# Taking 1/rms out of the input of a two-layer trunk's projections, on one Trainium2 core

## The reference, cut to what matters

```
h    = x * rsqrt(mean(x*x, axis=-1) + eps) * norm_w      # RMSNorm: one factor per row
proj = h @ w_in                                          # 1024 x 4160
p_rwkv, p_conv, p_moba, p_ret = split(proj)
y_rwkv = rwkv7_time_mix(...) * silu(gate)                # shifts p by one row, mixes, tanh/sigmoid
y_conv = B * conv3(C * h) * silu(gate)                   # three projections multiplied
y_moba = block attention(q, k, v) * silu(gate)           # softmax, T5 bias
y_ret  = retention(q, k, v), scaled by its own rms, * silu(gate)
x = x + concat(y) @ w_out                                # 1024 x 1024
```

## Time and profile before

| | |
|---|---|
| median of three executions | 649.53 us |
| the profiled execution: its own time | 649.84 us |
| its span, first to last instruction | 647.9 us |
| mean granted TensorE clock | 0.992 |
| TensorE matmul busy | 623.8 us (96%) |
| VectorE busy | 359.5 us (55%) |
| ScalarE busy | 255.0 us (39%) |
| GpSimd busy | 250.4 us (39%) |

### The profile page before, as it was taken

The page is one execution under the profiler, slowest core; times in us unless marked ns, Lnnn a source line. Parts: engine busy times, 40 slices in busy tenths (PEclk is TensorE's granted clock), DMA queues, the critical chain, the costliest instruction groups (busy, mean ns, idle before and its releaser), DMA issues.

```text
span 647.9 us, 11976 instructions
## 1 busy us (share of the span) xinstructions
PE 623.8 (96%) x4939; PEld 495.9 (77%) x4939; DVE 359.5 (55%) x615; ACT 255.0 (39%) x491; POOL 250.4 (39%) x192
## 2 busy tenths in 40 slices
PE   4999999999999999999999999999999999999994
PEld 3777878888877776878877787888787777687884
DVE  4838965441148557783262896645123765688433
ACT  4463422432135436443345442242213535534421
POOL 3663644315513123446515353431461313154620
PEclk9999999999999999999989999999999999999997
DMA  8775633327222121355543233241822122125503
GB/s 245 225 243 148 159 98 87 85 51 166 70 62 67 34 66 32 97 147 159 168 113 98 65 98 98 67 107 17 180 82 67 34 67 56 43 65 179 147 0 129
DMA packets 122615, 66.76 MB, mean 103 GB/s; under 512 B 31359, under 2 KB 115907, under 8 KB 122435
## 3 DMA queue, kind: packets, MB, share of 16 engines
q1 hardware_dynamic: 122562, 66.02, 37.8%
HBM read 55.78 MB, written 10.22 MB: 102 GB/s over the span
## 4 chain that ended last, share of the span: by engine, by line
PE 90%; DVE 3%; ACT 2%; DMA 2%; issue 1%; SPq 0%; DVEq 0%; ACTq 0%
PE bank L663 24%; PE bank L664 22%; PE bank L665 22%; PE bank L808 3%; PE bank L761 2%; PE bank L822 2%; PE bank L849 2%; DMA pages<-in_x_dram 2%; PE bank L833 1%; PE bank L775 1%; DVE act_lo L1339 1%; PE bank L933 1%; PE bank L968 1%; PE bank L864 1%; PE bank L984 1%
## 5 line engine op out<-in xcount | busy, mean ns | idle before, releaser
L595 POOL TENSOR_TENSOR w_lo<-w_raw,w_hi 128x512 fp32r<-128x512 f32 x164 | 226.3, 1403 | 314.2 <-ACT w_hi L1062 314.2
L663 PE MATMUL bank<-act_hi,w_hi 128*128 128x512 f32 x656 | 267.2, 407 | 1.8 <-DVE act_lo L1665 1.3
L665 PE MATMUL bank<-act_lo,w_hi 128*128 128x512 f32 x656 | 256.1, 390 | 0.0
L664 PE MATMUL bank<-act_hi,w_lo 128*128 128x512 f32 x656 | 256.1, 390 | 0.0
L663 PEld LDWEIGHTS bank<-act_hi,w_hi 128*128 128x128 f32 x656 | 123.1, 188 | 40.7 <-issue 14.5
L665 PEld LDWEIGHTS bank<-act_lo,w_hi 128*128 128x128 f32 x656 | 123.1, 188 | 26.6
L664 PEld LDWEIGHTS bank<-act_hi,w_lo 128*128 128x128 f32 x656 | 123.4, 188 | 23.9 <-issue 1.4
L1062 ACT ACTIVATE w_hi<-w_raw 128x512 fp32r<-128x512 f32 x142 | 81.3, 622 | 51.4 <-PE bank L665 47.4
L1151 ACT ACTIVATE pages<-bank 128x512 f32<-128x512 f32 x24 | 14.4, 598 | 111.6 <-PE bank L665 111.6
L588 POOL TENSOR_TENSOR w_hi<-w_raw,constants 128x512 fp32r<-128x512 f32 x22 | 23.4, 1085 | 58.0 <-DMA w_raw<-in_w_in_dram 46.2
L1676 DVE TENSOR_TENSOR x_or_y<-x_or_y,bank 128x512 f32<-128x512 f32 x16 | 11.0, 688 | 37.6 <-PE bank L665 37.6
(11 more groups left out here) (178 smaller groups left out, 726.9 us busy)
## 6 DMA issues: line engine op xcount, KB each, us to landing
w_raw<-in_w_in_dram SPq DMA_DIRECT2D x66, 512.0 KB, 4.1
w_raw<-in_w_out_dram SPq DMA_DIRECT2D x16, 512.0 KB, 3.9
x_scratch<-x_or_y SPq DMA_DIRECT2D x16, 256.0 KB, 4.6
x_or_y<-x_scratch SPq DMA_DIRECT2D x16, 256.0 KB, 2.7
pages<-in_x_dram SPq DMA_DIRECT2D x4, 512.0 KB, 8.9
out_dram<-pages SPq DMA_DIRECT2D x4, 512.0 KB, 4.0
bias_scratch<-pages SPq DMA_DIRECT2D x1, 1280.0 KB, 7.4
constants<-in_consts_dram SPq DMA_DIRECT2D x1, 1064.5 KB, 6.5
```

The costliest lines, as they stand in the source:

```text
L595: ins = pool.tensor_tensor(w_lo[:, i % LO, k, :], w_raw[:, i % RAW, k, :], w_hi[:, i % HI, k, :].bitcast(F32), ALU.subtract)
L663: mm(b[:, :], hi, act_hi[:, k, :], start=n == 0, stop=False)
L664: mm(b[:, :], lo, act_hi[:, k, :], start=False, stop=False)
L665: ins = mm(b[:, :], hi, act_lo[:, k, :], start=False, stop=n == KT - 1)
```

## The change

The split tiles hold x * norm_w instead of x * norm_w * rn; every projection is multiplied by rn behind TensorE.

- The split (first layer): ScalarE writes act_hi, and VectorE act_lo, straight from the transposed tiles in PSUM, as soon as those are there. `keep_warm` is gone. The rms broadcast runs inside the k pair, ahead of its last products, and ScalarE copies it to SBUF (`rn`, a tile of its own).
- Between the layers: inside the step of out7, ScalarE and VectorE split x tiles 0 to 6 for the next layer while out7's matmuls run (out7 now takes its products in the order 0 to 7, and each frees its act tile); VectorE's 7 subtractions stand ahead of its addition of out7 in its list. The `stat` matmuls run inside the next k pair, after its fifth product.
- Behind the projections, a new VectorE instruction multiplies shift, gate, ch and cb tiles in PSUM, in place, ahead of their other readers: those tiles have 3 readers instead of 2. Tiles rq, rk, mk and cc are copied with that factor by VectorE and no longer by ScalarE. mq, mv and rv go on as plain ScalarE copies; their factor is put in the score scale (`q_scale`), in the copy of the transposed rows (8 instructions in place of 2), and in `k_decay_rms`.
- The steps `mix` and `gate_out` hold what `shift` and `gate` did last on VectorE.
- The constant `chunk_reset` (512 columns of 128 partitions) is no longer loaded; two memsets write it.

More of the change, by code:

```diff
@@ L226, in bank_jobs @@
         elif kind == "gate":
[L227 removed]
+            proj(f"{step[1]}_g{step[2]}", 3)
         elif kind == "kk_square":
@@ L383, in trunk_kernel @@
         mean_sq, root, rms = small[:, 8:12], small[:, 12:16], small[:, 16:20]
+        q_scale, k_decay_rms = small[:, 28:32], small[:, 32:48]
+        chunk_reset = half(13, 0)
         UW = pages[:, 21 * PG:21 * PG + 2048].rearrange("p (m x i) -> p m x i", m=MATS, x=2)
@@ L623, in _, with stat_both @@
                         end(ins, f"x_in{m}", -1)
+            def stat_both(layer):
+                stat(layer, False)
+                stat(layer, True)
             def stat(layer, last):
@@ L679, in project, with rms_row @@
                             product(job, n)
[L681 to L688, removed]
+                def rms_row():
                     pe.wait_ge(s("rms"), layer + 1)
@@ L1042, in _, with square_rows @@
                 .then_inc(done("norm_cols", -1), 1)
-            for t in range(NT):
+            def square_rows(t):
                 act.wait_ge(s(f"x_loaded{t}"), 16)
@@ L1166, in to_rows @@
                                 act.wait_ge(*read(f"ret_ms{1}", layer))
-                            go(rows[what][:, :, p * P:(p + 1) * P], src.rearrange("p (t c) -> p t c", t=NT), ACT.Copy).then_inc(done(job, layer), 1)
+                                for t in range(NT):
+                                    ins = go(rows[what][:, t, p * P:(p + 1) * P], src[:, t * P:(t + 1) * P], ACT.Copy, scale=rms[:, t:t + 1])
+                                ins.then_inc(done(job, layer), 1)
+                            else:
+                                go(rows[what][:, :, p * P:(p + 1) * P], src.rearrange("p (t c) -> p t c", t=NT), ACT.Copy).then_inc(done(job, layer), 1)
                 def inverse_x(n):
@@ L1331, in _ @@
             for layer in range(DEPTH + 1):
[L1332 to L1350 removed]
+                def norm():
                     if layer == 0:
                         derive()
+                    dve.wait_ge(s("rms"), layer + 1)
+                    ts(q_scale, rms, N ** -0.5, None, ALU.mult).then_inc(s("row_factors"), 1)
+                    tt(k_decay_rms.rearrange("p (h t) -> p h t", h=HEADS), const("k_decay").rearrange("p (h t) -> p h t", h=HEADS),
+                       rms.unsqueeze(1).to_broadcast([P, HEADS, NT]), ALU.mult).then_inc(s("row_factors"), 1)
                 def derive():
@@ L1679, in project_out @@
                             evacuate_row(n)
-                run = dict(norm=norm, shift=shift, kk_norm=kk_norm, decay_scan=decay_scan, factors=factors, bonus=bonus,
+                run = dict(norm=norm, shift=shift, mix=mix, copy=copy, gate_out=gate_out, kk_norm=kk_norm, decay_scan=decay_scan, factors=factors, bonus=bonus,
                            gate=gate, scores=scores, block_rows=block_rows, inverse_y=inverse_y, inverse_yt=inverse_yt, rotate=rotate,
```

138 lines of the change are left out of this document (79 added, 59 removed).

## The result

The changed kernel takes 660.56 us in the median (659.34 to 662.07, 4 runs) beside 649.75 (648.99 to 651.33, 4 runs) for the kernel before: ratio 1.0164 with a 95% interval of 1.0136 to 1.0193. It is slower, by 1.4 to 1.9%. Its profiled execution took 662.07 us with a span of 660.1; the span before was 647.9, so 12.2 us have to be found in the trace, of which 1.5 belong to this execution alone (it is that much above its median).

The account below looks back on a forecast made before the run. TensorE, its matmuls filling 96% of the span, was taken as the bound. Start -0.8, seam -1.7, mixing +10.1 and layer ends +1.6 gave +9.2 us on 649.84, 659.0; set against the median, 658.8 us, range 653.5 to 664.

Parts of the forecast that it names:

- Start: First k pair: begins earlier, but k1 waits for its low weights until 20.35 us; pair ends at 32.1, gain 0.8 us.
- Seam: Between the layers: k0 waits for out7's addition behind seven subtractions, TensorE still for 3.1 us; gain 1.7 us.
- then the pair 10.9: Layer 1's k pair, after out7's addition at the seam: takes 10.9 us.
- Mixing: Time-mixing part: VectorE late for banks, stalls of 1.05, 2.4, 0.85 and 0.75 us; 5.05 us a layer, 10.1 in both.
- lasts 5.07 as before: Time-mixing part: decay_scan starts at 60.7 us behind the lora tanh and takes 5.07 us, as before, until 65.8.
- Price of a multiplication: VectorE's added in-place multiplications in PSUM: 0.7 us each, ends 0.6 and 1.06.
- Rival C: VectorE's multiplications are dearer or cheaper than 0.7 us: 656 to 663 us, inside the range; no separate chance given.
- End of a layer: cb0, cb1, conv_g0 and conv_g1: added multiplications delay the split ahead of out0; cost 0.8 us a layer, 1.6 in both.
- Costed at nothing: Copies taken from ScalarE, mv's row copies, q_scale, k_decay_rms, memsets, block_rows, SP's weight loads: each under 1 us if uncovered.
- B: Time mixing: VectorE's chain is not late for banks 1 and 0, part costs under 1 us; 645 to 648 us, chance 0.08.
- D: Time mixing: only one of two large stalls comes, ScalarE's tanh not held up; about 654 us, chance 0.1.
- A: New idle stretches drop TensorE's clock: one drop 660.5 us, at most 0.45; three about 664; two or more 0.15.

Follow-up runs that it names:

- the eighth kernel: The changed kernel with the constant 0.125 in place of q_scale in the scores, leaving out the 1/rms of q: one run, 659.59 us.
- the whole repaired change: The changed kernel with VectorE's mixing list reordered, out7's addition after three subtractions and six idle passes at the start: 649.25 us, 0.9983 of the kernel before.
- the first kernel: The changed kernel with the seven shifted tiles multiplied into SBUF instead of in place, freeing PSUM after one reader: 667.12 us, ratio 1.0267.
- the fourth kernel: The changed kernel with ScalarE's four lora tanh moved ahead of its part of r1: one run, 665.14 us.

## Why the prediction was right

I said 658.8, 653.5 to 664.0, and 660.56 was measured. The sum came out from terms that were nearly all off, in both directions.

**Start: -0.8 said, +0.86 measured.** The pair's first product is at 17.34 (said 17.4) and k1's at 20.31 behind the low weights (20.35). In the execution of the eighth kernel, which has this start and kept the clock there, wa comes 0.98 us earlier than before. What I had only as a rival is the clock drop, 1.6 us.

**Seam: -1.7 said, +1.07 measured.** The mechanism is the one said: seven subtractions, then the addition. From the first to the addition behind them are 5.69 us instead of 5.2, and the idle is 3.6 instead of 3.1; that is the first subtraction's 1.78 us beside GpSimd, the others took the step that I had said. The failed step is "then the pair 10.9": it ran partly at half clock, 2.5 us. I had the drop at the seam of before in front of me and gave one drop at most 0.45 and more than one 0.15; two came.

**Mixing: 5.05 a layer said, 3.50 measured.** The four places are right: v1 0.89 (said 1.05), g0 1.57 (2.4), g1 0.33 (0.85), rq0 0.61 (0.75), rq1 0.10. The chain is right up to decay_scan, which starts 28.5 us behind the pair's end (said 28.6) and behind the held-up tanh. The step that failed is "lasts 5.07 as before": scaling and scans took 4.28 us. The scans are as long as before (3.39 us, 3.31 before); the scaling took 0.86 and not the 1.80 of the earlier trace rows, since GpSimd's pair ended 0.31 us after its start, while before it ran beside all of it (59.99 to 62.98). Likewise factors 0 took 4.48 and not 5.08: its first two instructions took 0.53 and 0.54 us with GpSimd still, 1.25 and 1.52 before. I had copied durations that a neighbour had stretched to a place where the neighbour stands elsewhere.

**Price of a multiplication: 0.7 said, 0.695 measured** (38 instructions in place in PSUM). Rival C falls away. Its upper end of 1.06 (5.29 / 5) was the mean of two kinds: three of those five subtractions took 0.68 us, the two that met GpSimd 1.79 and 1.78. The page's fifth part:

```profile
L1414 DVE TENSOR_TENSOR bank<-bank,one_over_rms 128x512 f32<-128x512 f32 (+1 forms) x38 | 26.3, 695 | 23.7 <-PE bank L679 23.2
```

**End of a layer: 0.8 said, 0.6 measured.**

**Costed at nothing: +1.2 us in layer 0 and +0.8 in layer 1.** I had looked at when block_rows' results are loaded, not at what stands behind it in VectorE's list: the multiplication of retention's second gate, then ScalarE's tanh of it and two weight splits, then the rows that TensorE needs for mq1, 0.7 us late (L970 waits for L1194). The other part, 0.53 in both layers, is the product beside GpSimd above. In layer 1 mq1 is only 0.13 us late, and 0.25 more, from cc0 to cc1, stay open.

**Rivals.** B (VectorE's chain not late) and D (one large stall only) did not come: both large stalls are there. A came with two drops, at 1.6 and 2.5 us. That it and the things costed at nothing were in part made up by a mixing term that was too large is luck: -3.1 (mixing, two layers), +1.7 and +2.8 (start and seam), +2.0 (costed at nothing), -0.4 (layer ends) is +2.9 before rounding on the sum of 9.2, and the profiled execution stands 1.5 above the median. What was right without luck is the sign and where the time went: over half of the 12.1 us lies in the mixing part, at the four places named. Bonus is at 90.00 us (said 90.1).

## What to carry to other kernels

A scale moved behind a linear step is not free because the engine that now applies it is half idle. It makes one more link between the bank's last matmul and its release, and where that engine works off a list without gaps, the tiles there pay (3.5 us over five tiles here, nothing for the many tiles where it waited); look at that stretch of its timeline and at the order of the list before counting its work. When banks are late, reorder the list before copying data out of PSUM: the copy moved the wait and made the readers dearer. And before rebuilding a seam to save its microseconds, see what the clock does in it: a handful of small matmuls in the waits of the kernel before gave as much as the whole repaired change.

## What was not expected of the hardware

A drop of TensorE's clock outlasts its cause, and its length changes from one execution to the next. Behind the wait for k1's weights, with the start's instructions unchanged, the clock stood at half rate for 3.4 us in three executions, for 6.8 in one and not at all in two. At the seam, behind 3.6 us of idle, it fell each time: for 6.8 us in three executions, where the changed kernel's pair lost 2.5 us by it, and for 3.4 in two.

VectorE's time for an instruction with two SBUF inputs depends on GpSimd beside it: 0.68 to 0.75 us alone, 1.71 and 1.77 when it started well before the end of a GpSimd instruction, 1.19 when it started near that end. It looks like waiting and not like a slower pace: in the four rows shown above (two mix instructions of the first kernel, L1713 in both layers) the VectorE instruction ends 0.54 to 0.56 us behind the end of GpSimd's pair, whenever it had started. The seam's first subtraction does too (328.53 against 327.98). The scaling of one SBUF tile did the same, 0.86 against 1.66 us, so a single SBUF input is no safe sign; the mixes and multiplications that read PSUM stayed at 0.7. GpSimd loses as well: its pair of weight splits takes 2.53 us beside VectorE instructions on PSUM and 3.64 to 4.46 beside its chain on SBUF. So where ScalarE's weight splits came 1.7 us sooner, in the fourth kernel, durations changed in two other engines.
